# Linear attention in a two-layer trunk: its tiles placed among the latent heads, one product for both directions

## What is computed

```python
u = split_cols(h @ w_in[l], IN_COLS)
y_a, yc_a = gla_branch(...)   # linear attention, 4 heads, chunks of 64 tokens, forward and backward
y_b, yc_b = mla_branch(...)   # latent attention, 6 heads, keys 96 wide
y_c, yc_c = gqa_branch(...)   # grouped-query attention, 6 heads
x = x + gate[:, None, :] * (jnp.concatenate([y_a, y_b, y_c], axis=-1) @ w_out[l])
...
q_dec = qc * jnp.exp(cum)
k_inv = kc * jnp.exp(-cum)
o_inter = jnp.einsum('bnchk,bnhkv->bnchv', q_dec, s_prev)
a = jnp.einsum('bnihk,bnjhk->bnhij', q_dec, k_inv)
a = jnp.where(mask, a, 0.0)
o_intra = jnp.einsum('bnhij,bnjhv->bnihv', a, vc)
...
o = rms_norm(o_fwd + jnp.flip(o_bwd, axis=1), norm_w)
return o.reshape(z.shape) * jax.nn.silu(z)
```

## Time and profile before

| | us |
|---|---|
| median of three runs | 1039.66 (1039.33 to 1041.62) |
| the profiled execution | 1039.05, span 1036.9 |
| TensorE busy | 960.7 (93%) |
| VectorE busy | 510.0 (49%) |
| ScalarE busy | 420.5 (41%) |
| GpSimd busy | 136.9 (13%) |
| mean granted clock | 0.974 |

### The profile page before, as it was taken

One profiled execution on the slowest core, in us unless ns is written; L12 is line 12 of the kernel. 1 busy time (PEld: TensorE's weight loads), 2 busy tenths in 40 slices (PEclk: granted clock), 3 DMA queues, 4 the chain that ended last, 5 costly groups with the idle time before them and its releaser, 6 DMA issues.

```text
span 1036.9 us, 12558 instructions
## 1 busy us (share of the span) xinstructions
PE 960.7 (93%) x4563; PEld 667.0 (64%) x4563; DVE 510.0 (49%) x873; ACT 420.5 (41%) x755; POOL 136.9 (13%) x158
## 2 busy tenths in 40 slices
PE   4899999998999999999899889899998999999896
PEld 3587889886555554555488677688765545445485
DVE  4456443444843544655542654443647444555544
ACT  5435343212115445576901523433321254555802
POOL 1110000002340001000920100000022301000720
PEclk9899999999989999999999899899999899999998
DMA  9640312204001322040043111321322000022022
GB/s 346 240 115 23 82 41 62 62 22 162 1 1 48 116 82 82 1 153 10 17 159 92 62 47 36 81 62 42 102 87 76 1 0 1 1 82 81 1 102 82
DMA packets 67867, 74.12 MB, mean 71 GB/s; under 512 B 6148, under 2 KB 47456, under 8 KB 67680
## 3 DMA queue, kind: packets, MB, share of 16 engines
q1 hardware_dynamic: 61392, 60.17, 18.3%
q0 software_dynamic: 4016, 12.77, 3.4%
q10 hardware_dynamic: 2400, 0.38, 0.2%
HBM read 69.11 MB, written 4.19 MB: 71 GB/s over the span
## 4 chain that ended last, share of the span: by engine, by line
PE 82%; DVE 7%; ACT 5%; issue 4%; POOL 1%; ACTq 1%; DVEq 0%; POOLq 0%
PE pv L1719 10%; PE bank L1506 9%; PE bank L1507 9%; PE bank L1508 8%; PE bank L1770 6%; PE bank L1680 4%; PE bank L1801 3%; PE bank L1802 3%; PE bank L1803 3%; PE bank L1647 2%; PE bank L1627 2%; PE bank L1696 2%; PE bank L1549 2%; PE bank L1550 2%; PE bank L1548 2%
## 5 line engine op out<-in xcount | busy, mean ns | idle before, releaser
L1506 PE MATMUL bank<-hA_parts,W_parts 128*128 128x512 f32 (+1 forms) x496 | 181.3, 365 | 8.6 <-DVE h_low_parts L1037 5.9
L1507 PE MATMUL bank<-hA_parts,W_parts 128*128 128x512 f32 (+1 forms) x496 | 174.7, 352 | 0.0
L908 ACT ACTIVATE hA<-bank 128x512 f32<-128x512 f32 (+1 forms) x168 | 92.5, 561 | 82.2 <-PE bank L1770 56.1
L1313 DVE TENSOR_REDUCE mxp<-bank 128x1 f32<-128x384 f32 x192 | 96.5, 550 | 47.4 <-PE bank L1680 47.1
L1506 PEld LDWEIGHTS bank<-hA_parts,W_parts 128*128 128x128 f32 x496 | 95.3, 192 | 27.8 <-issue 11.1
L1508 PE MATMUL bank<-h_low_parts,W_parts 128*128 128x512 f32 (+1 forms) x310 | 109.2, 352 | 0.0
L1507 PEld LDWEIGHTS bank<-hA_parts,W_parts 128*128 128x128 f32 x496 | 95.3, 192 | 13.5 <-issue 2.2
L1719 PE MATMUL pv<-hA,vg 128*128 128x512 f32 (+1 forms) x168 | 83.1, 576 | 6.8 <-ACT hA L908 6.4
L1719 PE MATMUL pv<-hA,XA 128*128 128x512 f32 (+1 forms) x168 | 81.0, 563 | 2.4 <-ACT hA L908 2.3
L1044 DVE TENSOR_TENSOR W_parts<-W,W_parts 128x1024 fp32r<-128x1024 f32 x44 | 53.5, 1221 | 32.0 <-ACT W_parts L635 31.9
L1331 DVE SCALAR_TENSOR_TENSOR hA<-pv,hA 64x512 f32<-64x512 f32 (+1 forms) x36 | 21.6, 599 | 90.8 <-ACT hA L851 90.6
(11 more groups left out here) (261 smaller groups left out, 1834.1 us busy)
## 6 DMA issues: line engine op xcount, KB each, us to landing
W<-in_w_in SPq DMA_DIRECT2D x39, 512.0 KB, 4.0
W<-in_w_mod SPq DMA_DIRECT2D x8, 2048.0 KB, 8.0
W<-in_w_out SPq DMA_DIRECT2D x4, 2048.0 KB, 7.8
gqk<-in_w_mod SPq DMA_DIRECT2D x2, 1536.0 KB, 9.2
cqkv<-in_w_mod SPq DMA_DIRECT2D x2, 1536.0 KB, 13.7
XA<-in_x SPq DMA_DIRECT2D x4, 512.0 KB, 7.1
XA<-in_x POOLq DMA_DIRECT2D x4, 512.0 KB, 6.7
x_between_layers<-XA POOLq DMA_DIRECT2D x4, 512.0 KB, 2.9
```

What stands on the lines that cost most here:

```text
L908: act.activation(prob[slot % 4][:, 0:nq], ps("sc", l, h, q0, kt)[:, 0:nq], ACT.Exp, scale=MLA_SCALE if h < MLA_H else GQA_SCALE)\
L1313: dve.tensor_reduce(mxp[:, t, half:half + 1], ps("mx", l, h, q0, t, half)[:, 0:384], AX, ALU.max).then_inc(*up("part_max", l, h, q0, t, half))
L1506: pe.matmul(p[:, 0:c[1]], high[:, k, :], h_hi[:, k, toks], start=(k == 0), stop=False)
L1507: pe.matmul(p[:, 0:c[1]], low[:, k, :], h_hi[:, k, toks], start=False, stop=False)
```

## The change

- *One product for both directions.* Both triangles now go into one matrix `Ab[t % 2]`. The backward mask leaves the diagonal out. GpSimd then doubles the diagonal (`two_diagonals`, a product with a constant `twofold`, of ones with twos on the diagonal), and TensorE multiplies the matrix with the values once. The score products stay one a direction.
- *A tile with each latent head.* Only the first tile's score products stay in front. In the loop of head h, TensorE makes the state and value products of tile h behind the first unit's scores, the turn of the former tile behind the second's, and the score products of the next tile in unit 2 (layer 0) or 1 (layer 1). ScalarE copies the tile out at unit 1 and takes the roots at unit 3 (`o_root`).
- *GpSimd* takes the spreading of the queries from VectorE (`gla_in`: two operations for queries, two for states), for the first tile ahead of the last gate unit, for the others behind the rounding of the keys. Its large fill is now of 1024 columns, and the ones beside the values are set in six pieces.
- *The values* come right behind the first tile's score products, three tiles before and three behind head 0's maxima; ScalarE copies them, not VectorE.
- *VectorE's order in a head*: rope, normalising of the former head, square and sum of tile h, gate of the former tile, modulation sums, both masks of the next tile, then the maxima, with the normalising of the head's context output behind the two context maxima and the scaling of tile h behind the fourth reduction of latent scores.
- *Layer 1*: the item "ga2" stands behind "ss1l" (`seq_of`); layer 0 keeps it.
- *Memory*: `qbd`, `Ab`, `Sbd` and `vm` lie in other places, the constants have 128 more columns.

```diff
@@ -71,2 +71,10 @@

+def seq_of(layer):
+
+    if layer == 0:
+        return SEQ
+    rest = [item for item in SEQ if item != "ga2"]
+    i = rest.index("ss1l") + 1
+    return rest[:i] + ["ga2"] + rest[i:]
+
 UNITS = [("small", 0, ((0, GLA_A, 32), (64, MLA_KR, 32)))] + \
...
@@ -469,17 +480,10 @@

...
+                def gla_in(t):

-                pool.wait_ge(*at("con_in"))
-                for t in out_tiles(l):
+                    for d in range(2):
+                        if t - 1 in out_tiles(l):
+                            pool.wait_ge(*at("filled", "A", l, t - 1, d))
+                        pool.tensor_tensor(qbd[d], qd[d][:, t * P:t * P + P].unsqueeze(1).broadcast_to([P, 4, P]),
+                                           headed.unsqueeze(2).broadcast_to([P, 4, P]), ALU.mult)\
+                            .then_inc(*up("qbd", l, t, d))
                     for d in range(2):
@@ -492,7 +496,33 @@

+                def two_diagonals(t):

+                    pool.wait_ge(*at("A_masked", l, t, 1))
+                    pool.tensor_tensor(Ab[t % 2], Ab[t % 2], twofold.unsqueeze(1).broadcast_to([P, 4, P]), ALU.mult)\
+                        .then_inc(*up("A_both", l, t))
+
...
+                pool.wait_ge(*at("con_in"))
+                pool.wait_ge(*at("gla_factors", l, 1))
+                pool.memset(QK[:, 0:1024], 0.0).then_inc(*up("bd_zero", l))
+                pool.wait_ge(*at("filled", "kdT", l, 1, 1))
+                gla_in(out_tiles(l)[0])
+
+                pool.wait_ge(*at("Sbd", l, out_tiles(l)[0], 1))
+                pool.wait_ge(*at("filled", "F", l, "z7", LAT))
+                head_ones(0)
+                round_k(l, 0)
+                for t in range(TILES):
+                    if t == TILES - 1:
+                        pool.wait_ge(*at("zgate", l, len([c for j in range(8) for c in chunks_of("z", l)]) - 1))
+                    pool.memset(vm[t][:, :, 64:128], 1.0).then_inc(*up("vm_ones", l))
                 pool.wait_ge(*at("vm_ones", l))
+                pool.wait_ge(*at("round_k", l, 0))
+                two_diagonals(out_tiles(l)[0])
+                pool.wait_ge(*at("A_both", l, out_tiles(l)[0]))
                 head_ones(1)
@@ -512,2 +542,8 @@
                     round_k(l, h)
+                    if h < len(out_tiles(l)):
+                        pool.wait_ge(*at("round_k", l, h))
+                        gla_in(out_tiles(l)[h])
+                        pool.wait_ge(*at("Sbd", l, out_tiles(l)[h], 1))
+                        two_diagonals(out_tiles(l)[h])
+                        pool.wait_ge(*at("A_both", l, out_tiles(l)[h]))

@@ -692,3 +728,3 @@
                 zi = 0
-                for item in SEQ:
+                for item in seq_of(l):
...
@@ -778,2 +814,4 @@
                     let_go(("o", l, t), "o_copy", l, t)
+
+                def o_root(t):
                     act.wait_ge(*at("o_ss", l, t))
@@ -785,2 +823,11 @@

+                def mla_v(t):
+                    act.wait_ge(*at("vm_ones", l))
+                    act.wait_ge(*at("filled", "vp", l, t))
+                    src = ps("vp", l, t)[:, 0:384].rearrange("p (r e v) -> p r e v", r=3, e=2)
+                    for e in range(2):
+                        act.activation(vm[t][:, :, 128 * e:128 * e + 64], src[:, :, e, :], ACT.Copy)\
+                            .then_inc(*up("vm", l, t, e))
+                    let_go(("vp", l, t), "vm", l, t, 1)
+
                 def head_in(h):
@@ -887,4 +934,4 @@
                 round_q(0)
-                for t in out_tiles(l):
-                    o_out(t)
+                for t in range(TILES):
+                    mla_v(t)
                 slot = 0
...
@@ -918,2 +962,6 @@
                             gqa_in(h + 1, j + 1)
+                        if j == 1 and h < len(out_tiles(l)):
+                            o_out(out_tiles(l)[h])
+                        if j == 3 and h < len(out_tiles(l)):
+                            o_root(out_tiles(l)[h])
                         m = mod_of_head(l, h)
...
@@ -1216,3 +1254,5 @@
                         dve.wait_ge(*at("filled", "o", l, t - 2))
-                    dve.copy_predicated(Ab[t % 2][d], mask[d].unsqueeze(1).broadcast_to([P, 4, P]),
+                    if d:
+                        dve.wait_ge(*at("A_masked", l, t, 0))
+                    dve.copy_predicated(Ab[t % 2], mask[d].unsqueeze(1).broadcast_to([P, 4, P]),
                                         ps("A", l, t, d)[:].rearrange("p (h t) -> p h t", h=4))\
...
@@ -1295,3 +1325,22 @@

-                def maxima(h):
...
+                def maxima(h, tile=None, former=None):
                     if h >= 2:
@@ -1302,2 +1351,6 @@
                         for t in range(q0 // P, (q0 + nq) // P):
+                            if t == 2 and former is not None and len(qbs(l)) == 2:
+                                normalise(former, *qbs(l)[0][:2])
+                            if t == 4 and tile is not None:
+                                o_scale(tile)
                             if q0 == 0:
...
@@ -1359,23 +1393,5 @@
                 q_rope(0)
-                for t in [tiles[0]]:
-                    for d in range(2):
-                        a_in(t, d)
-                    for d in range(2):
-                        a_mask(t, d)
-                    for d in range(2):
-                        a_in(t + 1, d)
+                for d in range(2):
+                    a_mask(tiles[0], d)
                 maxima(0)
-                for t in tiles:
-                    if t + 1 < TILES:
-                        for d in range(2):
-                            a_mask(t + 1, d)
-                    if t + 2 < TILES:
-                        for d in range(2):
-                            a_in(t + 2, d)
-                    o_square(t)
-                    o_scale(t)
-                    if t - 1 in tiles:
-                        o_gate(t - 1)
-                o_gate(TILES - 1)
-                mla_v()
                 for h in heads:
@@ -1385,2 +1401,7 @@
                         normalise(h - 1, *qbs(l)[-1][:2])
+                    tile = tiles[h] if h < len(tiles) else None
+                    if tile is not None:
+                        o_square(tile)
+                    if 0 < h <= len(tiles):
+                        o_gate(tiles[h - 1])
                     m = mod_of_head(l, h)
@@ -1390,6 +1411,9 @@
                         low_parts(h + 1)
-                    if len(qbs(l)) == 2:
-                        normalise(h, *qbs(l)[0][:2])
+                    if h + 1 < len(tiles):
+                        for d in range(2):
+                            a_mask(tiles[h + 1], d)
                     if h + 1 < len(heads):
-                        maxima(h + 1)
+                        maxima(h + 1, tile, h)
+                    elif len(qbs(l)) == 2:
+                        normalise(h, *qbs(l)[0][:2])

...
@@ -1623,7 +1647,6 @@
                                       skip_group_check=True)
-                    for d in range(2):
-                        pe.wait_ge(*at("A_masked", l, t, d))
-                        for h in range(GLA_H):
-                            mm = pe.matmul(p[:, 64 * h:64 * h + 64], Ab[t % 2][d][:, h, :], glav[:, t, 64 * h:64 * h + 64],
-                                           start=False, stop=(d == 1), skip_group_check=True)
+                    pe.wait_ge(*at("A_both", l, t))
+                    for h in range(GLA_H):
+                        mm = pe.matmul(p[:, 64 * h:64 * h + 64], Ab[t % 2][:, h, :], glav[:, t, 64 * h:64 * h + 64],
+                                       start=False, stop=True, skip_group_check=True)
                     close(mm, "o", l, t)
@@ -1733,11 +1756,4 @@
                 gla_a(tiles[0])
-                maxes(max_groups(0))
-                for t in tiles:
-                    if t + 1 < TILES:
-                        gla_a(t + 1)
-                    gla_o(t)
-                    if t - 1 in tiles:
-                        gla_t(t - 1)
                 values(range(3))
-                gla_t(TILES - 1)
+                maxes(max_groups(0))
                 values(range(3, TILES))
@@ -1787,2 +1803,8 @@
                         flush(2)
+                        if j == 0 and h < len(tiles):
+                            gla_o(tiles[h])
+                        if j == 1 and 0 < h <= len(tiles):
+                            gla_t(tiles[h - 1])
+                        if j == MAX_FROM[l] - 1 and h + 1 < len(tiles):
+                            gla_a(tiles[h + 1])
                         if j >= MAX_FROM[l]:
@@ -1835,3 +1857,4 @@
     c[:, C_MF:C_MF + P] = same & (i[:, None] <= i[None, :])
-    c[:, C_MB:C_MB + P] = same & (i[:, None] >= i[None, :])
+    c[:, C_MB:C_MB + P] = same & (i[:, None] > i[None, :])
+    c[:, C_TWO:C_TWO + P] = 1.0 + np.eye(P)
     c[:, C_BD:C_BD + GLA_H] = i[:, None] // GLA_DK == np.arange(GLA_H)[None, :]
```

99 lines of the change are left out of this document (38 added, 61 removed).

## The result

The changed kernel takes 993.99 us (median of four, 992.4 to 994.95) beside 1040.64 us of the kernel before on the same chip: a ratio of 0.955, 95% interval 0.9528 to 0.9571. The profiled execution has a span of 992.9 us (before 1036.9) and a mean clock of 0.985 (before 0.974).

A forecast was written before the change was run, and what follows sets the result against it. TensorE was taken as full in the latent heads, but idle in part and at lower clock in the two stages. Terms 15.9 + 13.3 + 6.0 + 3.3 + 1.0 - 2.0 = 37.5 us off 1039.05, plus 0.6: 1002 us, range 992 to 1017.

The forecast's parts named there:

- The stages: Linear attention stages: 15.9 us less in layer 0, 13.3 in layer 1, net of tile work put into heads.
- The heads' price: Latent heads: each tile adds 2.32 us for state products, value products and turn, besides 1.87 for its score products.
- The waits covered: Layer 0's heads: inserted products cover TensorE waits of 0.89 us in two heads and 1.53 in another, 3.3 us less.
- The moved item: Layer 1's input projections: ga2 behind ss1l removes TensorE's 4.18 us wait and 2.4 of lower clock; taken as 6.0 less.
- VectorE's order: Heads: two context maxima ahead of normalising remove half of a 2.12 us TensorE wait for a bank, 1.0 us less.
- The new waits: Eight later tiles: TensorE waits on new GpSimd handoffs, 2 us more, with 10.8 us as the bound from above.
- all margins hold: Rival: all margins hold and the heads' waits go wholly, 996 to 999 us; chance 0.15 for 992 to 998.
- The pace set by GpSimd: Slower rival: GpSimd's late masked queries and states delay TensorE in eight heads, 1055 us; chance 0.03.
- the handoffs that return: Rival: TensorE waits 1.23 us in each of eight tiles, 10 us more, 1010 us; three such rivals 0.24 together.
- the mutual stop in every head: Rival: VectorE and GpSimd stop each other, 1.4 us per tile, 14 us, 1016 us; three such rivals 0.24 together.

The follow-up runs named there:

- the part undone: The changed kernel with layer 1's six ga2 exponentials put back ahead of the square of the latent key norm: 1001.2 us, ratio 0.9618.
- the part alone: The kernel before with one edit, ga2 behind the factors' norm in layer 1: 1034.48 us, ratio 0.9942.
- the order undone: The changed kernel with VectorE's normalising of the head's context output back in front of the maxima: 994.46 us, ratio 0.9561.
- the run without that wait: The changed kernel with VectorE's low parts of head 6's key ahead of the tile's square in layer 0's head 5: 991.39 us, ratio 0.9527.

## Why the prediction was right, and where its sizes were off

- *The stages.* The mechanism held: no idle time and clock 1.00 in both, 17.25 us left (19.2 forecast) and 15.84 (17.5). Most of the 2 us too much is one term. Ten maxima products: 4.3 us forecast, 2.82 measured (256.43 to 259.25), since I had their price from a row that ran at the lower level (columns as in the earlier trace rows, the clock is 0.50):

```profile
258.93:260.65 1.72, 1.72 (x5) 1.21 (x5) 1.72 (x5) 0.00 (x0) 0.00 (x0) 0.50 0.00 0
```

  The other terms came from rows at clock 1.00 and are off by a tenth or two: a pair of score products 1.87 forecast, 1.72 measured (251.13 to 252.85), the values 7.7 and 7.55, the first products 5.3 and 5.16.
- *The heads' price.* State and value products 1.93 forecast, 1.95 measured; the turn 0.39 forecast as its bound, 0.22 measured (387.22 to 387.44); with 1.72 for the scores a tile costs 3.9 us, and heads 1 and 3, which had no wait before, are 3.67 us longer. Here again the score products and the turn were too dear, 0.3 us per tile.
- *The waits covered.* I counted 3.3 us from three waits. Heads 2 and 4 pay 2.92 us instead of 3.67, 0.75 each less, where the modulation's row had a wait of 0.89. Head 0 pays 1.97: it had waits of 0.81 and 0.31 us before, which I had left out, and has none now. Head 5 gives back 1.0 of its 1.53 once its own new wait is away (18.12 us against 16.92 before, for 2.2 us of work). The two of head 0, in TensorE's timeline of the kernel before:

```profile
310.57 1.13 PE L1770 MATMUL bank<-hA 97*128 97x512 f32 x2 [0.31 <-DVE rt L1267]
...
312.51 0.70 PE L1719 MATMUL pv<-hA,XA 128*128 128x256 f32 x2 [0.81 <-ACT hA L908]
```

- *The moved item.* 6.0 us forecast, 6.26 in the profile, 6.9 with the part undone, 5.65 with the part alone. The split into 4.18 us of wait and 2.4 of clock is right: at the square the four products take 3.75 us behind the wait and 1.88 without.
- *VectorE's order.* 1.0 us forecast. Against the kernel before, heads 9 and 10 are 0.38 and 1.42 us shorter, and the way from the last head to layer 1's transposes is 2.0 us longer; with the order undone, the medians differ by 0.2 us. So the term came to about nothing. I had halved it for banks behind the same normalising, and the loss is elsewhere, at the output projection.
- *The new waits.* 2 us, put behind GpSimd. Behind GpSimd there are none, so the margins of 0.6 us and more held. What came instead are a wait of 2.1 us behind ScalarE's copy and VectorE's row in head 5, with 1.66 us of lower clock in the first profile, and 2.0 us at the output projection. The step that failed is the sentence that VectorE's own work on a tile "took at most 4.2 us with its waits", "out of a head in which it works 9.55 of 22.30 us": it counts busy time and not order. The square stands in VectorE's queue ahead of things that TensorE needs sooner, and in the one head where these are the low parts of a key, it shows. Together they took 5.1 us in the first profile (3.1 in head 5, by the run without that wait, and 2.0), where the term says 2.
- *The rivals.* That all margins hold (996 to 999) came nearest. The pace set by GpSimd (1055), the handoffs that return (1010), and the mutual stop in every head (1016) did not happen: heads without a tile are as long as before (14.46, 16.21 and 15.81 us against 14.47, 16.22 and 15.81), and heads with one pay TensorE's own price. The mutual stop is real, though: it lengthened VectorE's operations by 0.6 to 0.9 us in six heads with a tile without a wait of TensorE, and cost TensorE 1.5 us at the output projection, outside of the tiles.

The measured 44.0 us exceed the forecast 37.5 by 6.5. The stages' work was put too dear by 3.7 us and the heads by 4.9, some 3 of it the price of the ten tiles; the 2.0 us lost at the output projection go the other way. So the time lies in the range because the mechanism held in the stages and the heads, and its errors of size cancel in part.
